# A two-block sequence kernel: the opening computed by token halves, the f32 mean in two f32r passes, the ada columns in pairs

## The reference, cut to what matters

```python
h = rmsnorm(x, norm_mix)
q, k, v, r, lr_f, lr_b, u, g_a, g_b = split(h @ w_in)
log_a_f = log_sigmoid(lr_f @ w_decay_up_fwd + b_decay_fwd) / 16     # backwards likewise
o = gla_chunked(q, k, v, log_a_f) + gla_chunked reversed            # 4 heads
o = o * rsqrt(mean(o * o, -1) + EPS) * gla_norm * silu(r)
merged = sigmoid(g_a) * (o @ w_branch_gla) + sigmoid(g_b) * pooled branch of u
x = x + merged @ w_out
gate, up = split(rmsnorm(x) @ w_ffn_in);  x = x + (silu(gate) * up) @ w_ffn_out
mod = silu(c) @ w_ada            # for the second block: 24 columns of 128
```

## Time and profile before

| | us |
|---|---|
| median of 3 runs (1333.26 to 1333.56) | 1333.53 |
| the profiled execution, device time | 1334.0 |
| its span | 1332.2 |
| PE busy in the span | 1320.7 |
| mean granted clock of PE | 0.999 |

### The profile page before, as it was taken

How to read it: one execution, slowest core, us unless ns; L and a number is a source line. 1 busy time by engine, 2 the same in 40 slices (tenths; PEclk the granted TensorE clock), 3 DMA queues, 4 the chain that set the end, 5 groups by cost and what they waited for, 6 DMA issues and landing times.

```text
span 1332.2 us, 21030 instructions
## 1 busy us (share of the span) xinstructions
PE 1320.7 (99%) x8150; PEld 1094.2 (82%) x8150; DVE 717.3 (54%) x1273; ACT 572.6 (43%) x785; POOL 347.4 (26%) x97
## 2 busy tenths in 40 slices
PE   8999999999999999999999999999999999999998
PEld 6888989888888888888888878777788888888886
DVE  4643241664556666666744470222297778845336
ACT  5744352452343322222232242455665566654233
POOL 6421213224333000000144324332211112124341
PEclk9999999999999999999999999999999999999999
DMA  6232322224234455555433424323222322322321
GB/s 197 87 95 64 94 63 88 70 79 158 95 95 130 141 141 142 141 141 141 119 109 87 121 72 111 110 82 106 64 65 77 83 65 64 96 65 97 124 95 64
DMA packets 199636, 134.53 MB, mean 101 GB/s; under 512 B 5719, under 2 KB 190920, under 8 KB 199574
## 3 DMA queue, kind: packets, MB, share of 16 engines
q1 hardware_dynamic: 198342, 131.41, 33.7%
q10 hardware_dynamic: 848, 1.60, 0.3%
q0 software_dynamic: 384, 0.64, 0.2%
HBM read 131.51 MB, written 2.12 MB: 100 GB/s over the span
## 4 chain that ended last, share of the span: by engine, by line
PE 99%; DVE 1%; issue 0%; DMA 0%; ACT 0%; DVEq 0%; ACTq 0%
PE acc L484 22%; PE acc L485 22%; PE acc L486 22%; PE acc L493 3%; PE acc L495 3%; PE acc L494 3%; PE acc L508 1%; PE acc L507 1%; PE acc L509 1%; PE acc L2361 1%; PE acc L2508 1%; PE acc L2363 1%; PE acc L2506 1%; PE acc L2362 1%; PE acc L2507 1%; PE mid L2406 1%
## 5 line engine op out<-in xcount | busy, mean ns | idle before, releaser
L462 POOL TENSOR_TENSOR wlo<-raw,whi 128x2048 fp32r<-128x2048 f32 (+1 forms) x76 | 332.4, 4374 | 947.0 <-ACT whi L458 946.9
L484 PE MATMUL acc<-hhi,whi 128*128 128x512 f32 x896 | 355.0, 396 | 0.0
L485 PE MATMUL acc<-hlo,whi 128*128 128x512 f32 x896 | 349.1, 390 | 0.0
L486 PE MATMUL acc<-hhi,wlo 128*128 128x512 f32 x896 | 348.9, 389 | 0.0
L458 ACT ACTIVATE whi<-raw 128x2048 fp32r<-128x2048 f32 (+1 forms) x110 | 203.6, 1851 | 118.7 <-PE acc L486 100.7
L486 PEld LDWEIGHTS acc<-hhi,wlo 128*128 128x128 f32 x896 | 168.2, 188 | 35.6
L484 PEld LDWEIGHTS acc<-hhi,whi 128*128 128x128 f32 x896 | 168.3, 188 | 35.4 <-issue 1.9
L485 PEld LDWEIGHTS acc<-hlo,whi 128*128 128x128 f32 x896 | 168.4, 188 | 34.5 <-issue 1.2
L1251 DVE TENSOR_TENSOR wlo<-raw,whi 128x2048 fp32r<-128x2048 f32 (+1 forms) x33 | 74.2, 2249 | 20.8 <-ACT whi L458 20.8
L484 PE MATMUL acc<-ahi,whi 128*128 128x512 f32 x176 | 68.7, 390 | 0.0
L485 PE MATMUL acc<-alo,whi 128*128 128x512 f32 x176 | 68.5, 389 | 0.0
(11 more groups left out here) (395 smaller groups left out, 2303.9 us busy)
## 6 DMA issues: line engine op xcount, KB each, us to landing
raw<-in_w_in_dram SPq DMA_DIRECT2D x56, 512.0 KB
raw<-in_w_in_dram SPq DMA_DIRECT2D x26, 1024.0 KB
raw<-in_w_ffn_in_dram SPq DMA_DIRECT2D x44, 512.0 KB
ada<-in_w_ada_dram SPq DMA_DIRECT2D x24, 512.0 KB, 3.9
raw<-in_w_ffn_out_dram SPq DMA_DIRECT2D x16, 704.0 KB
raw<-in_w_out_dram SPq DMA_DIRECT2D x8, 1024.0 KB
xnat<-in_x_dram SPq DMA_DIRECT2D x8, 512.0 KB, 6.2
raw<-in_w_branch_gla_dram SPq DMA_DIRECT2D x4, 1024.0 KB
```

Of the source, the lines that this page charges most:

```text
L462: nc.gpsimd.tensor_tensor(wlo[:, slot, 0:n], raw[:, slot, 0:n], whi[:, slot, 0:n].bitcast(f32), ALU.subtract).then_inc(s_unit_lo, 1)
L484: nc.tensor.matmul(acc[bank][:, :], h, xh[:, k, :], start=(k == 0), stop=False)
L485: nc.tensor.matmul(acc[bank][:, :], h, xl[:, k, :], start=False, stop=False)
L486: last = nc.tensor.matmul(acc[bank][:, :], lo, xh[:, k, :], start=False, stop=(k == nk - 1))
```

## The change

It has four parts.
- The opening goes by halves of 256 tokens. The first weight pair is loaded between the second and the third x tile. POOL, not ACT, makes its high part, and its low part at once, ahead of its DMAs. x is transposed by halves into half banks (half_bank); ACT and DVE make high and low pieces of 256 tokens, and take turns on a bank. ACT squares x tiles 2 and 3. PE does the query and key products 256 wide in four lots, with two keep_clocks of 4 and 6 in place of 5 and 8, and the decay projection between them.
- In the decay chain ACT splits unit 3 before round 1, evicts queries and keys before round 2, splits unit 4 before round 5 and copies the first two gate tiles out before round 6; their sigmoid follows in place after the split of unit 5. decay(7) moves behind the first value tile.
- The mean over a head's 256 values takes two f32r passes: ACT copies the sum of squares to an f32r tile (gla_sum_hi), DVE subtracts the remainder, PE multiplies both by an f32r `mean_dv`. gla_sum_hi stands ahead of the split in the heads' loop, and ahead of gla_rs at j == 1 in the tail.
- In the feed-forward part PE does the two ada products of an iteration together, behind its second unit. SP's, ACT's and DVE's orders there stay as they are.

The diff, cut to its core, with the indentation of each piece taken off. HALF is 256. x_rms_done(3) becomes 11, and two later waits on `s_n_hi` and `s_n_lo` count 8 more.

```diff
@@ -131,7 +132,7 @@
 mean_dm = at("mean_dm", S0 + .5, [P, P])
-mean_dv = at("mean_dv", S0 + 4.5, [P, P])
+mean_dv = at("mean_dv", S0 + 4.5, [P, P], f32r)
 mean_p = at("mean_p", S0 + 5, [P, P])
@@ -184,6 +185,7 @@
 ex = at("ex", A0 + 70, [P, 3, L])
+exl, exh = at("exl", A0 + 70, [P, L], f32r), at("exh", A0 + 72, [P, L], f32r)
 kdT = at("kdT", A0 + 76, [P, 2, TT, P])
@@ -423,9 +425,11 @@
-def x_bank(k):
-    return acc[k] if k < 4 else M[k - 4]
+def half_bank(half, k):
+    b = k // 4 * 2 + k % 2
+    bank = M[b] if half == 0 else (acc[0], acc[3], M[0], M[1])[b]
+    return bank[:, k // 2 % 2 * HALF:(k // 2 % 2 + 1) * HALF]
@@ -473,7 +477,7 @@
 def raw_free(sp, u):
-    if later(u - 1):
+    if later(u - 2):
         sp.wait_ge(s_unit_lo, u - 1)
@@ -568,16 +572,19 @@
 for t in range(TT):
+    if t == TT // 2:
+        load_pair(1, 0, w_in, C_Q, C_K)
     sp.dma_start(xnat[:, t, :], xn[t]).then_inc(s_x_in[t], 16)
...
 def head_loads(h, u):
-    load_pair(u, 0, w_in, C_Q + h * DK, C_K + h * DK)
     if isinstance(u, int):
...
             row_load(sp, name, r)
+    else:
+        load_pair(u, 0, w_in, C_Q + h * DK, C_K + h * DK)
     load(u + 1, 1, kview(w_in, C_GA + h * 256, 256))
@@ -702,28 +709,44 @@
 act.wait_ge(s_consts, 1)
-for t in range(TT):
-    if t % 2 == 0:
-        act.wait_ge(s_x_in[t], 16)
-        A(nsq[:, :, :].rearrange("p a n -> p (a n)"), xnat[:, t, :], ACT.Square,
-          accum_out=xss[:, t:t + 1]).then_inc(s_x_rms, 1)
-        act.wait_ge(s_x_rms, x_rms_done(t) - 2)
-    else:
-        act.wait_ge(s_x_sq, t // 2 + 1)
+def x_square(t):
+    act.wait_ge(s_x_in[t], 16)
+    A(nsq[:, :, :].rearrange("p a n -> p (a n)"), xnat[:, t, :], ACT.Square,
+      accum_out=xss[:, t:t + 1]).then_inc(s_x_rms, 1)
+    act.wait_ge(s_x_rms, x_rms_done(t) - 2)
+def x_rs(t):
     A(xrs[:, t:t + 1], xss[:, t:t + 1], ACT.Ln, bias=eps_col[:, :], scale=1.0 / DM).then_inc(s_x_rms, 1)
...
     A(xrs[:, t:t + 1], xrs[:, t:t + 1], ACT.Exp, scale=-0.5).then_inc(s_x_rms, 1)
-    if t == 0:
-        act.wait_ge(s_col_mm, 1)
-        A(vcol[:, R_NM:R_NM + KT], M[0][:, 0:KT], ACT.Copy).then_inc(s_cols, 1)
+def half_hi(half, k, done, low):
+    act.wait_ge(s_x_tr, half * (KT // 2) + k // 4 * 2 + k % 2 + 1)
+    if k % 4 > 1:
+        act.wait_ge(low, k - 1)
+    A(hhi[:, k, half * HALF:(half + 1) * HALF], half_bank(half, k), ACT.Identity,
+      scale=vcol[:, R_NM + k:R_NM + k + 1]).then_inc(done, 1)
+x_square(0)
+x_rs(0)
+act.wait_ge(s_col_mm, 1)
+A(vcol[:, R_NM:R_NM + KT], M[3][:, 0:KT], ACT.Copy).then_inc(s_cols, 1)
+act.wait_ge(s_x_sq, 1)
+x_rs(1)
 act.wait_ge(s_cols, 1)
+for k in range(KT // 2):
+    half_hi(0, k, s_n_hi, s_n_lo)
+for t in range(TT // 2, TT):
+    x_square(t)
+    x_rs(t)
+for k in range(KT // 2, KT):
+    half_hi(0, k, s_n_hi, s_n_lo)
 for k in range(KT):
-    act.wait_ge(s_x_tr, k + 1)
-    A(hhi[:, k, :], x_bank(k)[:, :], ACT.Identity, scale=vcol[:, R_NM + k:R_NM + k + 1])\
-        .then_inc(s_norm_hi, 1)
-split_hi(act, 1, 0)
+    half_hi(1, k, s_norm_hi, s_norm_lo)
+act.wait_ge(s_unit_hi, 2)
+split_hi(act, 2, 1)
 act.wait_ge(s_col_mm, 2)
@@ -732,7 +755,6 @@
 A(brow[:, L:BW], M[2][0:A_HEADS, 0:BW - L], ACT.Copy).then_inc(s_bias_row, 1)
-split_hi(act, 2, 1)
 act.wait_ge(s_lr3, 1)
@@ -745,11 +767,17 @@
 for i in range(8):
-    if i == 4:
+    if i == 1:
+        split_hi(act, 3, 0)
+    if i == 2:
         head_evict_qk(0)
-        split_hi(act, 3, 0)
-    if i == 7:
+    if i == 5:
         split_hi(act, 4, 1)
+    if i == 6:
+        for c in range(2):
+            b, full, _ = TL(U_HEAD, 2 + c)
+            act.wait_ge(s_acc_full, full)
+            A(sig_ga[:, c, :], acc[b][:, :], ACT.Copy).then_inc(s_acc_free[b], 1)
     act.wait_ge(s_up_mm, i + 1)
@@ -813,6 +841,10 @@
+def gla_sum_hi(g):
+    act.wait_ge(s_gsq_sum, g * 2 + 1)
+    A(exh[:, :], ex[:, 0, :], ACT.Copy).then_inc(s_gsq, 1)
@@ -824,9 +856,12 @@
-head_evict_ga(0)
+head_split(0, 3)
+for c in range(2):
+    b, _, free = TL(U_HEAD, 2 + c)
+    act.wait_ge(s_acc_free[b], free + 1)
+    A(sig_ga[:, c, :], sig_ga[:, c, :], ACT.Sigmoid)
 head_evict_v(0)
-head_split(0, 3)
 head_evict_r(0)
@@ -839,6 +874,7 @@
 head_evict_v(h)
+gla_sum_hi(g)
 head_split(h, 3)
@@ -1306,18 +1343,24 @@
+def half_lo(half, k, ready, done):
+    dve.wait_ge(ready, k + 1)
+    hs = slice(half * HALF, (half + 1) * HALF)
+    V.scalar_tensor_tensor(hlo[:, k, hs], half_bank(half, k), vcol[:, R_NM + k:R_NM + k + 1],
+                           hhi[:, k, hs].bitcast(f32), ALU.mult, ALU.subtract).then_inc(done, 1)
...
 x_normalise(1)
-dve.wait_ge(s_x_sq, 1)
-x_square(3)
+dve.wait_ge(s_cols, 1)
+for k in range(KT // 2):
+    half_lo(0, k, s_n_hi, s_n_lo)
 x_normalise(2)
 x_normalise(3)
-dve.wait_ge(s_cols, 1)
+for k in range(KT // 2, KT):
+    half_lo(0, k, s_n_hi, s_n_lo)
 for k in range(KT):
-    dve.wait_ge(s_norm_hi, k + 1)
-    V.scalar_tensor_tensor(hlo[:, k, :], x_bank(k)[:, :], vcol[:, R_NM + k:R_NM + k + 1],
-                           hhi[:, k, :].bitcast(f32), ALU.mult, ALU.subtract).then_inc(s_norm_lo, 1)
+    half_lo(1, k, s_norm_hi, s_norm_lo)
@@ -1422,8 +1465,10 @@
 def gla_square_sum(g):
-    dve.wait_ge(s_gsq, g * 2 + 2)
+    dve.wait_ge(s_gsq, g * 3 + 2)
     V.tensor_tensor(ex[:, 0, :], ex[:, 0, :], ex[:, 1, :], ALU.add).then_inc(s_gsq_sum, 1)
+    dve.wait_ge(s_gsq, g * 3 + 3)
+    V.tensor_tensor(exl[:, :], ex[:, 0, :], exh[:, :].bitcast(f32), ALU.subtract).then_inc(s_gsq_sum, 1)
@@ -1875,6 +1920,9 @@
 pool.wait_ge(s_pool_prep, 3)
+pool.wait_ge(s_unit_in[0], 32)
+nc.gpsimd.tensor_copy(whi[:, 0, :], raw[:, 0, :]).then_inc(s_unit_hi, 1)
+split_lo(pool, 1, 0)
 pool.wait_ge(s_x_in[TT - 1], 16)
@@ -1892,7 +1940,6 @@
 pool.wait_ge(s_pool_prep, 5)
-split_lo(pool, 1, 0)
 split_lo(pool, 2, 1)
@@ -1988,54 +2035,70 @@
 pe.wait_ge(s_first_in, 32)
-nc.tensor.transpose(M[0][:, 0:KT], grow[:, :], ident[0:KT, 0:KT]).then_inc(s_col_mm, 1)
-for t in range(TT):
-    keep_clock(x_bank(KT - 1), (17, 0, 5, 0)[t])
+nc.tensor.transpose(M[3][:, 0:KT], grow[:, :], ident[0:KT, 0:KT]).then_inc(s_col_mm, 1)
+b_q, _, _ = TL(U_HEAD, 0)
+b_k, _, _ = TL(U_HEAD, 1)
+b_lr, _, _ = TL(U_LR, 0)
+def x_transposes(t):
     pe.wait_ge(s_x_n, t + 1)
     for k in range(KT):
-        if t == 0 and k == 4:
+        if t == 0 and k == 5:
             pe.wait_ge(s_cols, 1)
-        last = nc.tensor.transpose(x_bank(k)[:, t * P:(t + 1) * P], xnat[:, t, k * P:(k + 1) * P],
-                                   ident[:, :])
-        if t == TT - 1:
+        if t == 2 and k == 4:
+            pe.wait_ge(s_n_lo, 4)
+        last = nc.tensor.transpose(half_bank(t // 2, k)[:, t % 2 * P:(t % 2 + 1) * P],
+                                   xnat[:, t, k * P:(k + 1) * P], ident[:, :])
+        if t % 2 and k % 4 > 1:
             last.then_inc(s_x_tr, 1)
+def first_hi(half, k0, k1):
+    hs = slice(half * HALF, (half + 1) * HALF)
+    for k in range(k0, k1):
+        pe.wait_ge(s_norm_lo if half else s_n_lo, k + 1)
+        for bank, j in ((b_q, 0), (b_k, 1)):
+            h = whi[:, 0, k * 2 * P + j * P:k * 2 * P + (j + 1) * P]
+            mm(acc[bank][:, hs], h, hhi[:, k, hs], start=(half == 0 and k == 0), stop=False,
+               skip_group_check=True)
+            mm(acc[bank][:, hs], h, hlo[:, k, hs], start=False, stop=False, skip_group_check=True)
+def first_lo(half):
+    hs = slice(half * HALF, (half + 1) * HALF)
+    for bank, j in ((b_q, 0), (b_k, 1)):
+        for k in range(KT):
+            lo = wlo[:, 0, k * 2 * P + j * P:k * 2 * P + (j + 1) * P]
+            last = mm(acc[bank][:, hs], lo, hhi[:, k, hs], start=False, stop=(k == KT - 1),
+                      skip_group_check=True)
+        if half:
+            last.then_inc(s_acc_full, 1)
+keep_clock(acc[b_lr], 17)
+x_transposes(0)
+x_transposes(1)
+keep_clock(acc[b_lr], 4)
+pe.wait_ge(s_unit_hi, U_HEAD + 1)
+first_hi(0, 0, KT // 2)
+keep_clock(acc[b_lr], 6)
+x_transposes(2)
+x_transposes(3)
+first_hi(0, KT // 2, KT)
+pe.wait_ge(s_unit_lo, U_HEAD + 1)
+first_lo(0)
+first_hi(1, 0, KT // 2)
 pe.wait_ge(s_lr_in, 32)
-b, _, _ = TL(U_LR, 0)
 strips = P // LR
-pe.wait_ge(s_norm_lo, 1)
-keep_clock(acc[b], 8)
 for m in range(KT // strips):
...
             k = m * strips + c
-            last = mm(acc[b][c * LR:(c + 1) * LR, :], wlr[:, k, :], h[:, k, :].bitcast(f32),
+            last = mm(acc[b_lr][c * LR:(c + 1) * LR, :], wlr[:, k, :], h[:, k, :].bitcast(f32),
                       start=(m == 0 and h is hhi), stop=(m == 1 and h is hlo), skip_group_check=True)
-    if m == 0:
-        pe.wait_ge(s_rows_in, 12 * 16)
-        nc.tensor.transpose(acc[3][:, 0:P], vrow[:, :], ident[:, :]).then_inc(s_col_mm, 1)
-    if m == 1:
-        last.then_inc(s_acc_full, 1)
-def first_hi(bank, j):
-    for k in range(KT):
-        h = whi[:, 0, k * 2 * P + j * P:k * 2 * P + (j + 1) * P]
-        mm(acc[bank][:, :], h, hhi[:, k, :], start=(k == 0), stop=False)
-        mm(acc[bank][:, :], h, hlo[:, k, :], start=False, stop=False)
-def first_lo(bank, j):
-    for k in range(KT):
```

(38 more changed lines are left out.)

## The result

The changed kernel takes 1365.7 us (median, 1364.6 to 1369.7) against 1333.4 us of the kernel before on the same chip: ratio 1.0247, interval 1.0233 to 1.0261. It is slower, as forecast, but by 32 us instead of 11, and outside the range. The profiled execution is the slowest of the six (1369.7 us, span 1367.9).

The account below looks back on a forecast made before the run. PE was taken as the bound, busy for 99% of the span. Opening and decay chain +0.1, three means -1.2, fourth mean +3.5 and pairing +9.0 summed to +11.4 us: 1345 us, with 8 in 10 for 1336 to 1351.

Parts of the forecast that it names:

- Opening: Up to the first gate tile: PE reaches that tile at 33.7 us, 1.5 us earlier than 35.17.
- ACT squares both ... so DVE has them normalised at 14.7 and 16.2: Opening: ACT squares the third and fourth x tiles, 1.7 us each; DVE has them normalised at 14.7 and 16.2.
- Decay chain: ACT's split ahead of round 1 delays the second scan to 41.0; PE waits 1.6 us for it at decay(5).
- Mean, three heads: Two f32r passes save 0.4 us a head, the added ACT and DVE work being hidden: -1.2 us in all.
- Mean, fourth head: Tail: PE waits 3.9 us for ACT's split and copy and DVE's subtraction, less 0.4 saved: +3.5 us.
- the subtraction (0.7 ...): Fourth head's mean: DVE's subtraction takes 0.7 us after ACT's copy and hand-over and ends at 280.15.
- Pairing: Feed-forward loop: the later second weight pair makes PE wait 1.8 us per two iterations, +9.0 us over ten.
- with 0.1 for landing: Feed-forward loop: 0.1 us for landing, within 24.2 us from ada(2i-2) to the sum that ada(2i+1) needs.
- a tie, no term: Feed-forward loop: second unit's low half ready 11.35 us after the trigger, wanted at 11.4, so no cost counted.
- The upper bound named there: Feed-forward loop: if a load takes 8.2 us, the waits come to 15 us.
- By the rows, +11.4, which I keep: PE's clock: no slowdown counted after the 3.9 us wait; by the skill's rule the sum would be +13.4.
- A: Rival: clock falls at the 3.9 us wait, +2, and loads land later, up to +6: 1347 to 1353; chance 0.15.

Follow-up runs that it names:

- (5): Changed kernel with SyncE issuing both weight pairs of a feed-forward iteration ahead of both ada loads, PE's order still paired: 1344.1 us.
- (7): Changed kernel with keep_clock products put ahead of the fourth head's mean, in PE's wait: 1367.7 us with 56, 1363.0 us with 32.
- (6): Changed kernel with SyncE waiting for the second unit's weight pair to land before issuing the next ada load and pair: 1363.1 us.

## Why the forecast was right and wrong

- **Opening.** PE's own work (16.6 us) was right, and the weight pair's landing was near (POOL starts on it at 10.42, forecast 10.0). The step that failed is "ACT squares both ... so DVE has them normalised at 14.7 and 16.2": it priced DVE alone, while the same section of the forecast put POOL's low half beside it. It comes to +0.8 instead of -1.5 at the first gate tile. With the low half out of the way the tile comes at 33.86, the forecast's 33.7.
- **Decay chain.** 1.46 us instead of 1.6, right in cause and size.
- **Mean, three heads.** The means come 2.56, 2.11 and 1.66 us late in turn: -0.45 a head, forecast -0.4.
- **Mean, fourth head.** Place and releaser were right. The step that failed is "the subtraction (0.7 ...)", 4.57 beside POOL. With POOL held the wait is 3.73, the forecast's 3.9. The trace of before could have told. Its DVE and POOL timelines have this pair, where the operation's like takes 0.71:

```profile
262.04 4.02 DVE L1471 TENSOR_TENSOR ptmp<-upad 128x527 f32<-128x527 f32 x1
```

```profile
260.88 4.61 POOL L462 TENSOR_TENSOR wlo<-raw,whi 128x2048 fp32r<-128x2048 f32 x1 [3.56 <-ACT whi L458]
```

The first ends 0.57 us after the second, as in the changed kernel.
- **Pairing.** The mechanism was right (5) and the ada waits of 8.3 us stand against 9.0. The steps that failed are "with 0.1 for landing" (0.85 from the last bytes to the engine) and from it "a tie, no term". The forecast's own terms (7.0 + 0.1 + 2.0 + 2.29) make 11.39 and not 11.35, against 11.4 wanted, so nothing was to spare. The pair came after 7.9 to 8.6 us (9.7 in the first iteration) and so the low half 0.8 us late or more: one wait of 0.3 to 0.9 in each of four rounds and one of 2.2 in the first, 5.0 us in all. The upper bound named there (landing after 8.2 us, 15 us in all) would have held the waits of 13.3, but not the clock behind them.
- **The clock.** "By the rows, +11.4, which I keep" was the wrong choice. After the tail's wait the clock is at its lower level for 13 products, 2.7 us (7), against the 2.0 estimated from the start. By the rule that I weighed, of the Trainium skill, "TensorE: Matmul & The Clock Gate", HAM oscillation — how this bites in real kernels, the next work after a long enough gap starts slow. The trace agrees there. But the forecast put the risk at one gap. Four waits of 1.6 to 2.2 us in the loop were also followed by products at the lower level, 1.6 us each. "Through waits of up to 1.0 us" in the earlier trace rows was no evidence on them.
- **Rivals.** A had the direction of the miss (a low clock, a late load) at 0.15. Both its prices were too small, and its cause for the late load, two sets queued together, is worth 0 to 0.6 us a pair (6). It missed DVE and POOL altogether, and so did every other case; the range had no place for 20 us.

By size, at the fourth mean, the opening and the loop of the profiled execution: DVE behind POOL 3.7 + 2.2, the late landing and its restarts 9.1 (5.0 + 4.8, less the 0.7 that the ada waits fell short), the clock 2.7 + 6.5. They make 24.2, and with the forecast's 11.4 35.6; the profiled span has 35.7 over before (1367.9 against 1332.2). The 4.8 is itself a remainder, so that the sum closes tests the terms outside the loop and not those in it. The split within the loop is reckoned from one trace and not tested term by term. At the median the loop costs 3 us less than in it.

## What to carry to other kernels

When an operation is put beside another engine's, take its duration from a row where that engine does the same, above all for DVE beside GpSimd when both work on SBUF alone. A load that is queued behind a wait for a product costs its traffic and also the time to its semaphore: read that from when the consumer starts, not from where the rate falls. And an engine whose new waits are short but many should be priced with its clock, or the queue be put in another order so that there are none: here one line did it.
